# Norms, and the units around them, in halves of the tokens; the attention's branch in three split passes behind that of the matrix memory

## The reference, cut to what matters

```
xn   = RMSNorm_pre(x);  cols = xn @ w_in          # columns of three mixers A, B, C and of 3 x 1024 gates
h_a  = matrix memory (mLSTM) of A's columns       # chunkwise
h_b  = sliding-window attention of B's columns
h_c  = RWKV-7 delta rule of C's columns           # recurrent over chunks of 64 tokens
merged = sum over b of sigmoid(gate_b) * (h_b @ w_branch_b)
x   += RMSNorm_post(merged @ w_out)
xn   = RMSNorm_pre(x)
x   += RMSNorm_post((silu(xn @ w_gate) * (xn @ w_up)) @ w_ffn_out)
```

## Time and profile before

| | |
|---|---|
| median of 3 runs | 2446.35 us (2445.53 to 2447.68) |
| the profiled execution | 2449.73 us |
| its span, first to last instruction | 2447.9 us |
| mean granted clock of TensorE | 0.977 |
| PE busy in the span | 2335.9 us (95%) |
| VectorE, ScalarE, GpSimd busy | 994.4, 863.1, 786.7 us (41%, 35%, 32%) |

### The profile page before, as it was taken

One profiled execution on the slowest core, in us unless ns is written; L12 is line 12 of the kernel. 1 busy time (PEld: TensorE's weight loads), 2 busy tenths in 40 slices (PEclk: granted clock), 3 DMA queues, 4 the chain that ended last, 5 costly groups with the idle time before them and its releaser, 6 DMA issues.

```text
span 2447.9 us, 53310 instructions
## 1 busy us (share of the span) xinstructions
PE 2335.9 (95%) x23450; PEld 2224.4 (91%) x23450; DVE 994.4 (41%) x1559; ACT 863.1 (35%) x1442; POOL 786.7 (32%) x630
## 2 busy tenths in 40 slices
PE   7999989999999899999989999999999989999997
PEld 7998878988899899999989988888888989999997
DVE  4435654454434522220073376455443624332102
ACT  4345532213344522222244455222313544222222
POOL 3432322112235244444424332221212433444441
PEclk9999989999999999999989999999999999999998
DMA  5432211111124132233325221112113242332331
GB/s 164 128 88 74 57 40 32 28 49 32 42 69 145 58 90 87 87 91 87 83 93 136 61 74 53 32 28 49 32 28 83 68 129 61 90 92 87 88 88 52
DMA packets 334190, 180.80 MB, mean 74 GB/s; under 512 B 33528, under 2 KB 330648, under 8 KB 332936
## 3 DMA queue, kind: packets, MB, share of 16 engines
q1 hardware_dynamic: 333776, 177.34, 26.1%
q10 hardware_dynamic: 184, 0.05, 0.0%
HBM read 167.98 MB, written 9.38 MB: 72 GB/s over the span
## 4 chain that ended last, share of the span: by engine, by line
PE 82%; DVE 11%; ACT 4%; issue 2%; DMA 1%; POOL 0%; DVEq 0%; ACTq 0%; SPq 0%; POOLq 0%
PE psum_products L658 72%; PE psum_mixer L658 8%; DVE xn_low L2050 1%; DMA w_raw<-in_w_in 1%; DVE merged L2044 1%; DVE squares L1641 1%; DVE gate_product L2042 1%; DVE xn_low L1638 0%; ACT c_in_rate L1222 0%; ACT w_high L1222 0%; ACT c_kprime L1222 0%; DVE c_kappa_r L1753 0%; DVE c_in_rate L1754 0%; ACT L1222 0%; PE psum_mixer L1037 0%
## 5 line engine op out<-in xcount | busy, mean ns | idle before, releaser
L2273 POOL TENSOR_TENSOR w_low<-w_raw,w_high 128x512 fp32r<-128x512 f32 (+2 forms) x606 | 761.8, 1279 | 1557.7 <-ACT w_high L1222 1557.1
L658 PE MATMUL psum_products<-xn_high,w_high 128*128 128x272 f32 (+1 forms) x3424 | 738.6, 297 | 28.8 <-DVE xn_low L1623 12.3
L658 PE MATMUL psum_products<-xn_high,w_low 128*128 128x272 f32 (+1 forms) x3424 | 710.7, 289 | 0.0
L658 PE MATMUL psum_products<-xn_low,w_high 128*128 128x272 f32 (+1 forms) x3424 | 708.9, 289 | 0.0
L658 PEld LDWEIGHTS psum_products<-xn_high,w_high 128*128 128x128 f32 x3424 | 542.9, 189 | 50.6 <-issue 26.2
L658 PEld LDWEIGHTS psum_products<-xn_low,w_high 128*128 128x128 f32 x3424 | 543.0, 190 | 0.0
L658 PEld LDWEIGHTS psum_products<-xn_high,w_low 128*128 128x128 f32 x3424 | 539.7, 190 | 0.0
L1222 ACT ACTIVATE w_high<-w_raw 128x1024 fp32r<-128x1024 f32 (+2 forms) x303 | 303.2, 1003 | 174.6 <-PE psum_products L658 144.3
L658 PE MATMUL psum_products<-hidden_high,w_high 128*128 128x272 f32 x704 | 145.9, 288 | 0.0
L658 PE MATMUL psum_products<-hidden_high,w_low 128*128 128x272 f32 x704 | 145.7, 288 | 0.0
L658 PE MATMUL psum_products<-hidden_low,w_high 128*128 128x272 f32 x704 | 145.1, 288 | 0.0
(11 more groups left out here) (374 smaller groups left out, 3008.9 us busy)
## 6 DMA issues: line engine op xcount, KB each, us to landing
w_raw<-in_w_in SPq DMA_DIRECT2D x112, 512.0 KB, 4.0
w_raw<-in_w_ffn_in SPq DMA_DIRECT2D x88, 512.0 KB, 3.8
w_raw<-in_w_ffn_out SPq DMA_DIRECT2D x32, 512.0 KB, 3.9
w_raw<-in_w_out SPq DMA_DIRECT2D x16, 512.0 KB, 4.0
w_raw<-in_w_ffn_out SPq DMA_DIRECT2D x16, 384.0 KB, 3.4
x_kept<-x SPq DMA_DIRECT2D x2, 2176.0 KB, 7.5
x<-x_kept SPq DMA_DIRECT2D x2, 2176.0 KB, 9.7
w_raw<-in_w_in SPq DMA_DIRECT2D x16, 256.0 KB, 3.9
```

The source lines that it names most:

```text
L658: return pe.matmul(out, lhsT, rhs, start=start, stop=stop, skip_group_check=True)
L2273: low_ready.inc(pool.tensor_tensor(wl[:, n % NSPLIT, ks_], wraw[:, slot, ks_], wh[:, n % NSPLIT, ks_].bitcast(F32), ALU.subtract))
```

## The change

1. **Boundaries in halves.** All boundaries but the last one (behind the last feed-forward) go by halves of the tokens. The two units ahead of a boundary (`mix` 6 and 7; the last two thirds of output unit 7) are ordered by `two_halves`: first both units for tokens 0 to 271, with their sums, then both for the rest. ScalarE evicts them by halves (`out_half`), and takes Ln and Exp for the first half alone. VectorE, ScalarE and PE then go through 14 steps (`STEPS`): blocks 0 to 5 of the first half, blocks 0 to 5 of the second, and blocks 6 and 7 for all tokens. The second half's eviction and Ln fall into step 2 on ScalarE, its Exp into step 3.
2. **Weights.** Five raw slots, four `w_high` slots; `w_low` is written over the raw tile, so a raw slot is free when the unit's products are done. Units are split up to four ahead. The splits that would fall on the two units ahead of a boundary come in step 12, on ScalarE and GpSimd; `split_both` is gone. The unit of A's gate columns loads 128 columns in place of 8.
3. **The attention's branch.** `gate_order` puts all of (0, m) before all of (1, m). When branch (0, 7) is done, `b_out_split` copies `b_heads` into A's `a_out_high` on ScalarE and subtracts in place on VectorE (`b_out_low`), 4 instructions each, and the branch's units run in three passes like the others. Their weights are split too.

```diff
-NRAW, NSPLIT = 3, 3
+NRAW, NSPLIT = 5, 4
...
-    return [(b, m) for m in range(KD) for b in range(2)] + [(2, m) for m in range(KD)]
+    return [(b, m) for b in range(3) for m in range(KD)]
...
+            products += [("b_out_split", l)] if (b, m) == (0, KD - 1) else []
...
-    return s[0] == "branch" and s[2] == 1
+    return False
...
+BY_HALF = 6
+BOTH = (0, 1)
+STEPS = [(k, (0,)) for k in range(BY_HALF)] + [(k, (1,)) for k in range(BY_HALF)] + [(k, BOTH) for k in range(BY_HALF, KD)]
+def halved(l, w_):
+    return w_ in (1, 3) and (l, w_) != (DEPTH - 1, 3)
+def steps_from(l, w_):
+    return [(k, BOTH) for k in range(KD)] if (l, w_) == (0, 0) else STEPS
+def by_halves(s):
+    return (s[0] == "mix" and s[2] >= KD - 2 and halved(s[1], 1)
+            or s[0] == "ffn_out" and s[2] == KD - 1 and s[3] >= 1 and halved(s[1], 3))
...
-    wl = fixed("w_low", [P, NSPLIT, 8, P], F32R)
+    wl = place("w_low", [P, NRAW, 8, P], wraw_at, F32R)
...
+    b_low = place("b_out_low", [P, 4, T], bh_at, F32R)
...
-                upto = sum(unit_no[t] <= u + (3 if s in split_no else 2) for t in split_units)
+                upto = sum(unit_no[t] <= u + 4 for t in split_units)
...
-                if plan[i + 1][0] == "norm_post":
-                    at_ = plan[i + 1]
+                if by_halves(s):
+                    at_ = ("midst", s[1] + (s[0] == "ffn_out"), 2 if s[0] == "mix" else 0)
...
-                return [cols(a["w_in"], 4 * A_W, A_H, 0), cols(a["w_in"], 4 * A_W + A_H, A_H, 32)]
+                return [cols(a["w_in"], 4 * A_W, 32, 0), cols(a["w_in"], 4 * A_W + A_H, 96, 32)]
...
-                        gemm(s, rhs=[bh[:, k, :] for k in range(4)], nk=4, steps=steps)
+                        gemm(s, rh=a_high, rl=b_low, nk=4, steps=steps)
...
-                bank[0].claim(pe)
-                bank[1].claim(pe)
-                for k in range(KD):
+                for i, (k, bs) in enumerate(steps_from(l, w_)):
                     for s in pair:
-                        product(s, 1)
-                    pe.wait_ge(sq_ready.sem, norm_base(l, w_) + k + 1)
-                    for b in range(2):
+                        product(s, 1, bs, late=(l, w_) != (0, 0))
+                    if i == 1 and (l, w_) != (0, 0):
+                        last_sum(*((l, 1) if w_ == 2 else (l - 1, 3)), 1)
+                    pe.wait_ge(sq_ready.sem, norm_base(l, w_) + i + 1)
+                    for b in bs:
+                        if k == 0:
+                            bank[b].claim(pe)
                         last = mm(mp[b][:, 0:HALF], C("ones"), squares[:, k, b * HALF:(b + 1) * HALF],
                                   start=(k == 0), stop=(k == KD - 1))
                         if k == KD - 1:
...
+            def two_halves(l, w_, one, two, nk):
+                one(8, (0,))
+                two(nk - 2, (0,))
+                post_sums(l, w_, (0,))
+                two(2, (0,))
+                one(3, (1,))
+                last_sum(l, w_, 0)
+                one(8, (1,))
+                two(nk - 2, (1,))
+                post_sums(l, w_, (1,), wait=w_ == 1)
+                two(2, (1,))
...
+            def factor_log(w_, b):
+                dst = rstd_of(w_)
+                bank[b].read(act, "act")
+                step(fn(dst[:, tokens((b,))], mp[b][:, 0:HALF], ACT.Ln, scale=1.0 / D, bias=C("scalars", 0, 1)), bank[b].empty["act"])
+            def factor_exp(w_, b):
+                dst = rstd_of(w_)
+                step(fn(dst[:, tokens((b,))], dst[:, tokens((b,))], ACT.Exp, scale=-0.5), flow("rstd"))
+            def out_half(s, b):
+                sq, y = (squares, mixed) if s[0] == "mix" else (sq2, ffn_y)
+                if b == 0:
+                    flow("first_half").wait_next(act, "act")
+                    pair = tiles[s[:3] if s[0] == "ffn_out" else s][0]
+                else:
+                    pair = product_done(s)
+                src = gp[:, 2 * pair + b, 0:HALF]
+                name = "last_squares" if b else "first_squares_1" if s[0] == "mix" else "first_squares_3"
+                (sq_ready if b and s[2] < KD - 1 else flow(name)).inc(fn(sq[:, s[2], tokens((b,))], src, ACT.Square))
+                step(fn(y[:, s[2], tokens((b,))], src, ACT.Copy), emptied["act"] if b else None)
+            def norm_post(l, w_):
+                if not halved(l, w_):
+                    factor(rstd_of(w_))
+                    return
+                factor_log(w_, 0)
+                factor_exp(w_, 0)
+                if w_ == 1:
+                    out_half(("mix", l, KD - 2), 1)
             def norm_pre(l, w_):
                 g0 = PARAM_AT["norm_mix_pre" if w_ == 0 else "norm_ffn_pre"]
                 hi = uh if w_ == 0 else xh
-                for k in range(KD):
+                post = (l, 1) if w_ == 2 else (l - 1, 3)
+                for i, (k, bs) in enumerate(steps_from(l, w_)):
+                    n = tokens(bs)
                     if l or w_:
                         flow("x_new").wait_next(act, "act")
-                    xh_ready.inc(fn(hi[:, k, :], x[:, k, :], ACT.Copy, scale=prm[:, l, g0 + k:g0 + k + 1]))
-                    sq_ready.inc(fn(squares[:, k, :], x[:, k, :], ACT.Square))
-                    if l == 0 and w_ == 0 and k < 3:
+                        if i == 2:
+                            out_half(("mix", l, KD - 1) if w_ == 2 else ("ffn_out", l - 1, KD - 1, 2), 1)
+                    xh_ready.inc(fn(hi[:, k, n], x[:, k, n], ACT.Copy, scale=prm[:, l, g0 + k:g0 + k + 1]))
+                    sq_ready.inc(fn(squares[:, k, n], x[:, k, n], ACT.Square))
+                    if l or w_:
+                        if i == 2:
+                            factor_log(post[1], 1)
+                        if i == 3:
+                            factor_exp(post[1], 1)
+                        if k == BY_HALF and bs == BOTH:
+                            for u in ahead.get(("midst", l, w_), ()):
+                                split_high(u)
+                    elif k < 4:
                         split_high(k)
                     if k == KD - 2:
                         log_table()
...
+            def b_out_high(l):
+                act.wait_ge(products.sem, unit_no[("branch", l, 0, KD - 1)] + 1)
+                for h in range(4):
+                    step(fn(a_high[:, h], bh[:, h, :], ACT.Copy), flow("b_out_high"))
...
-            def split_both(n):
...
-                step(dve.tensor_copy(wh[:, slot, 0:nk], raw))
-                step(tt(wl[:, slot, 0:nk], raw, wh[:, slot, 0:nk].bitcast(F32), SUB), vec_ready)
...
+                order = STEPS if halved(l, w_) else [(k, BOTH) for k in range(KD)]
+                second = order.index((0, (1,))) if halved(l, w_) else None
                 flow("rstd").wait_next(dve, "dve")
                 if w_ == 1:
                     dve.wait_ge(flow("x_back").sem, 16 * (l + 1))
-                def scaled(k):
-                    step(stt(out=tmp[:, k, :], in0=src[:, k, :], scalar=prm[:, l, g0 + k:g0 + k + 1], in1=rstd[:],
+                def scaled(i):
+                    k, bs = order[i]
+                    n = tokens(bs)
+                    if i == second:
+                        flow("rstd").wait_next(dve, "dve")
+                    step(stt(out=tmp[:, k, n], in0=src[:, k, n], scalar=prm[:, l, g0 + k:g0 + k + 1], in1=rstd_of(w_)[:, n],
                              op0=MUL, op1=MUL))
                 scaled(0)
-                for k in range(KD):
-                    step(tt(x[:, k, :], x[:, k, :], tmp[:, k, :], ADD), flow("x_new"))
-                    if k + 1 < KD:
-                        scaled(k + 1)
+                for i, (k, bs) in enumerate(order):
+                    n = tokens(bs)
+                    step(tt(x[:, k, n], x[:, k, n], tmp[:, k, n], ADD), flow("x_new"))
+                    if i == 0 and w_ == 1:
+                        h = tokens((1,))
+                        dve.wait_ge(sq_ready.sem, norm_base(l, 1) + KD - 1)
+                        step(tt(squares[:, 0, h], squares[:, 0, h], squares[:, KD - 2, h], ADD), flow("squares_added"))
+                    if i + 1 < len(order):
+                        if i + 1 != second:
+                            scaled(i + 1)
                         if after[0] < DEPTH:
-                            step_low(*after, k)
+                            step_low(*after, i)
+                        if i + 1 == second:
+                            scaled(i + 1)
...
+            def b_out_low(l):
+                for h in range(4):
+                    flow("b_out_high").wait_next(dve, "dve")
+                    step(tt(b_low[:, h, :], bh[:, h, :], a_high[:, h].bitcast(F32), SUB), flow("b_h") if h == 3 else None)
...
-                    s = units[u]
-                    if s in split_no:
-                        wait_low(sp, split_no[s])
-                    else:
-                        sp.wait_ge(products.sem, unit_no[s] + 1)
+                    sp.wait_ge(products.sem, u + 1)
...
```

(39 more changed lines are left out.)

123 lines of the change are left out of this document (68 added, 55 removed).

## The result

The changed kernel takes 2473.83 us (median of 4 runs, 2469.32 to 2474.79) where the kernel before took 2447.01 beside it: a ratio of 1.0099, 95% interval 1.0084 to 1.0113. It is slower by 1.0%. The forecast was 2453.5 with a range of 2436 to 2466: the direction was right, the size was not, and the time lies 8 us above the range. The profiled execution took 2474.69, with a span of 2472.9, a mean granted clock of 0.969 (0.977 before) and PE busy for 2346.1 us (2335.9 before).

A forecast was written before the change was run, and what follows sets the result against it. PE was taken as the bound nearly everywhere, so gains had to come from its waits, slow restarts or work. Boundaries +8.7 and C −1.5 made +7.2 us: 2453.5 us against a median of 2446.35, range 2436 to 2466.

The forecast's parts named there:

- +8.7: Three halved boundaries together: 8.7 us longer, +5.7 from the step sums and +3.0 from slow restarts.
- The pace: Boundaries: half steps of 1.64 us plus late splits and tables end the steps later, +5.7 us over three.
- The slow restarts: Boundaries: PE restarts at a lower clock behind the 3.1 us wait in step 13; 1.0 per boundary, +3.0.
- Per layer −4.25 + 3.0 − 2.5 + 1.5 + 0.5 + 1.0: C per layer: passes, lost fillers, fillers moved into preparations (−2.5), weight splits, `b_out_split`, buffers; −0.75 us.
- the buffers' +1.0: C per layer: `w_low` waits go, the `c_kprime` wait grows to some 3.3 us, a slow restart follows; +1.0 us.
- −4.25 for cheaper passes: C per layer: three passes save 1.15 us in k-steps run alone, 3.1 in fillers, nothing in preparations.
- +1.5 and +0.5: C per layer: splitting the branch's eight units costs 1.5 us, `b_out_split`'s copies and subtractions 0.5.
- +3.0 for PE without fillers in the third group: C per layer: three levels without filler lose 0.75 us each, the Gram matrices 0.7; +3.0.
- The first, cheap half operations: Rival, chance 0.13: VectorE's 272-column operations take 0.36 and 0.39 us, three boundaries give −5.3; 2439.5 us.
- The second, C by PE's work: Rival, chance 0.19: C follows PE's work, so the branch's 18.3 us saving comes through, less 1; 2438 us.
- The third, the clock within the steps: Rival, chance 0.10: the clock falls within the half steps at boundaries, 9.5 us each, 28 in all; 2482 us.

The follow-up runs named there:

- busy_waits_in_halves: `halves_only` plus throw-away PE products ahead of four of each boundary's late blocks; 2457.54 us, ratio 1.0038 to the kernel before.
- halves_only: The changed kernel with the attention's branch as before (one pass, old order, no input split); halves and deeper buffers stay; 2460.56 us, ratio 1.0050.
- order_alone: The changed kernel with the branch's new order but in one pass, without `b_out_split`; 2468.47 us, ratio 1.0087 to the kernel before.
- gates_first: The changed kernel with one gate unit per layer moved ahead of the branch unit that can't be cut up as filler; 2463.18 us, ratio 1.0069.
- whole_norms: The changed kernel with whole norms and whole last units; its branch and deeper buffers stay; 2464.40 us, ratio 1.0075 to the kernel before.
- four_halves: The changed kernel with four blocks in halves, not six, and four whole blocks behind them; 2470.05 us, ratio 1.0089 to the kernel before.
- buffers_alone: The changed kernel with norms, last units and branch as before, leaving only the deeper weight buffers and their split places; 2451.66 us, ratio 1.0015.
- idle_products_before: The kernel before, with throw-away PE products filling the gap at each of three boundaries; 2444.58 us, ratio 0.9988.

## Why the prediction was wrong

**Boundaries: right, the number in part by luck.** The mechanism and each time on the way came as worked out, and so did the sum: +8.7 forecast; 8.9 in the profile, 8.9 and 9.4 in the medians. The pace is 5.5 in `busy_waits_in_halves` (forecast +5.7). The slow restarts, forecast at +3.0, were sized too small: 5.2 in `halves_only`. They were sized behind one late step; there are two such places, and the one behind the second half's Ln and Exp I had counted as lateness alone. In the changed kernel's profile the first boundary ran at 1.00 throughout and came out 1.0 longer; with the same halves, `halves_only`, `order_alone`, `gates_first` and its kernel of one pass have 9.9 to 10.8 over the three stretches, and that of two passes 14.3.

**The branch: the failed step.** "Per layer −4.25 + 3.0 − 2.5 + 1.5 + 0.5 + 1.0" was the sum. Without the buffers' +1.0 it says -1.75 per layer, where 6.4 to 6.6 were measured. Two terms of it are wrong. The first is the −4.25 for cheaper passes. The prediction granted that fillers in preparations save nothing, but let those in Gram matrices, levels and chains save 3.1 and those by themselves 1.15; with their splits (+1.5 and +0.5) three passes should have gained 2.25 per layer. On the order of `gates_first` they gained nothing (2463.18 against 2462.55 with one pass, whose units lie at other places), and 8.1 us of work less per layer moved the median by 1.7. The saving did arrive in the third and fourth group and was lost again in the fifth, at a lower clock; the prediction priced each saving where it is made and followed it no further.

The second is the +3.0 for PE without fillers in the third group. The exchange of two units gives 5.3 per layer back by the medians, and 6.9 and 6.2 in that group. I had priced the levels without fillers by their waits (0.75 each, and waits of 0.86 came) but not the stretch of 25 us, with a clock of 0.50 to 0.94, that follows when PE runs out of fillers at the end of the preparation ahead of it: 4.2 and 2.7 of these us.

These two don't make up the whole distance. In the profiles of the three kernels with this plan (the change, `whole_norms`, `four_halves`) against the four with the buffers and the old branch, the third group of a layer is 3.6 us longer in the mean, the fifth 2.6, the second 1.6, the fourth 1.4, and the first 1.9 shorter. What lengthens the second, fourth and fifth stays open.

**The buffers.** +1.0 per layer in C was forecast, by a longer wait for `c_kprime` and a slow restart; the longest wait grew to 3.4 (`buffers_alone`), but C did not get longer (0.4 to 5.4 shorter in three profiles, the same in the fourth): this term is wrong too. The 4.3 us lie in the second layer's projections instead. There every kernel here is 2 to 6 us longer than the one profile of the kernel before, `idle_products_before` included, which has none of the change (4.6, at a granted clock of 0.97 where before had 0.99). So it may be that profile that is short there; what the buffers cost by themselves stays open.

**The rivals.** The first, cheap half operations, is refuted by their rows (0.442, 0.502). The second, C by PE's work, wanted two thirds of the work to arrive; between three and two passes, the clean pair, 3.4 of 16.2 us did, so it is refuted as a rule for C, though it held within the third group. The third, the clock within the steps, was half true: not through all the half steps, but in a stretch behind two waits of 1.2 us and again at the last step, behind one of 2.3. The Trainium skill (TensorE: Matmul & The Clock Gate, A second HAM failure mode: psum-queue depth-cycling) has frequent short idles between groups of matmuls make the clock swing. `halves_only` agrees (0.98, then 0.50 behind the two waits), and so does `busy_waits_in_halves` (1.00 where they are filled). The first boundary of the changed kernel had the same waits (1.19 and 1.22) and stayed at 1.00, so the waits alone don't decide it.

## What to carry to other kernels

Making a filler of another engine's chain cheaper need not be a gain: 16.2 us less of such work moved the time by 3.4 here. Ask of each saved instruction whether it lay on the path or under a wait, and what the engine does with the time behind it. Before you reorder fillers, look for the one unit that can't be cut up, and where it blocks the queue of those behind it; one exchange of two units was worth 5.3 us per layer here. When you take a step out of a plan to isolate another, see that what is left keeps its place. And price a wait of PE by what follows it at the lower clock as well as by its length: filling the gap with throw-away products gave 0.12% where halving the norms lost 0.4%.

## What the runs showed of the hardware that I had not expected

The same instructions with nearly the same waits met different clocks: the half steps of the first boundary ran at 1.00 in the changed kernel and at 0.50 for 6 us in `halves_only`, and the stretch came out 1.0 and 3.7 us longer than before. And with one pass of the branch less, C's last group, which had less work for PE, came out longer, at a granted clock of 0.84 and 0.81 where it had been 0.96 and 0.94.
